# The input product of the odd layer by seven block products instead of eight

## The reference, cut to what matters

```python
h = rmsnorm(x, norm_w[layer])
proj = h @ od_w_in[i]                    # 1024 x 3088
q, k, v, r, a_lr = split_cols(
    proj, [GLA_K_WIDTH, GLA_K_WIDTH, GLA_V_WIDTH, GLA_V_WIDTH, GLA_GATE_RANK])   # 512, 512, 1024, 1024, 16
c_out = gla_mixer(q, k, v, a_lr, gla_w_a2[i], gla_b_a[i], gla_norm[i]) * jax.nn.silu(r)
x = x + c_out @ od_w_out[i]
```

## Time and profile before

| | |
|---|---|
| time, 3 runs | 1682.04 us median, 1680.92 to 1682.89 |
| span of the profiled execution | 1680.7 us, 22631 instructions (no other time of that execution is recorded) |
| granted TensorE clock, mean | 0.998 |
| TensorE / VectorE / ScalarE / GpSimd busy | 98% / 49% / 38% / 17% |
| DMA | 236.18 MB, 141 GB/s |

### The profile page before, as it was taken

The page is one execution under the profiler, slowest core; times in us unless marked ns, Lnnn a source line. Parts: engine busy times, 40 slices in busy tenths (PEclk is TensorE's granted clock), DMA queues, the critical chain, the costliest instruction groups (busy, mean ns, idle before and its releaser), DMA issues.

```text
span 1680.7 us, 22631 instructions
## 1 busy us (share of the span) xinstructions
PE 1643.8 (98%) x7898; PEld 1330.3 (79%) x7898; DVE 822.9 (49%) x1671; ACT 633.7 (38%) x1616; POOL 281.0 (17%) x516
## 2 busy tenths in 40 slices
PE   6999999999999999999999999999999999999998
PEld 4777788777777678888778888888888888878886
DVE  6744545667666574533552333334334443354443
ACT  6522334666666562323450222222222232132221
POOL 3883000000000332100000112222222121000110
PEclk9999999999999999999999999999999999999999
DMA  5466544455444865222243323423332332276663
GB/s 217 146 182 190 152 153 134 142 170 149 146 148 134 262 177 200 83 93 95 79 151 107 114 96 110 129 98 114 115 110 88 129 110 75 94 246 192 189 189 110
DMA packets 224520, 236.18 MB, mean 141 GB/s; under 512 B 53368, under 2 KB 169752, under 8 KB 224408
## 3 DMA queue, kind: packets, MB, share of 16 engines
q1 hardware_dynamic: 221752, 233.07, 43.7%
q10 hardware_dynamic: 2656, 1.67, 0.4%
HBM read 140.12 MB, written 94.57 MB: 140 GB/s over the span
## 4 chain that ended last, share of the span: by engine, by line
PE 92%; DVE 3%; ACT 2%; DMA 2%; issue 1%; SPq 0%; POOL 0%; DVEq 0%; ACTq 0%; POOLq 0%
PE bank L1232 23%; PE bank L2196 22%; PE bank L2246 10%; PE score_banks L2196 8%; PE bank L2355 8%; PE score_banks L2355 2%; PE bank L2305 2%; PE bank L2302 2%; PE bank L2303 2%; PE score_banks L2284 1%; PE score_banks L1288 1%; PE bank L1315 1%; PE bank L1269 1%; PE bank L1261 1%; PE bank L1305 1%
## 5 line engine op out<-in xcount | busy, mean ns | idle before, releaser
L1232 PE MATMUL bank<-ht_hi,ev_w_hi 128*128 128x512 f32 x576 | 239.7, 416 | 2.4 <-DVE ht_lo L944 2.4
L2196 PE MATMUL bank<-ht_hi,odd_w_hi 128*128 128x512 f32 x576 | 239.1, 415 | 0.0
L1232 PE MATMUL bank<-ht_hi,ev_w_lo 128*128 128x512 f32 x576 | 226.4, 393 | 0.0
L1232 PE MATMUL bank<-ht_lo,ev_w_hi 128*128 128x512 f32 x576 | 226.2, 393 | 0.0
L2196 PE MATMUL bank<-ht_lo,odd_w_hi 128*128 128x512 f32 x576 | 225.5, 392 | 0.0
L2196 PE MATMUL bank<-ht_hi,odd_w_lo 128*128 128x512 f32 x576 | 224.1, 389 | 0.0
L1232 PEld LDWEIGHTS bank<-ht_hi,ev_w_hi 128*128 128x128 f32 x576 | 108.8, 189 | 38.7 <-issue 17.1
L1972 DVE COPY odd_stage<-bank 128x512 f32<-128x512 f32 x72 | 49.8, 691 | 168.9 <-PE bank L2196 168.9
L1232 PEld LDWEIGHTS bank<-ht_lo,ev_w_hi 128*128 128x128 f32 x576 | 108.6, 189 | 24.9
L2196 PEld LDWEIGHTS bank<-ht_lo,odd_w_hi 128*128 128x128 f32 x576 | 108.1, 188 | 24.1
L2196 PEld LDWEIGHTS bank<-ht_hi,odd_w_hi 128*128 128x128 f32 x576 | 108.3, 188 | 23.1 <-issue 3.0
(11 more groups left out here) (320 smaller groups left out, 3337.7 us busy)
## 6 DMA issues: line engine op xcount, KB each, us to landing
odd_gl_in<-scr_heads SPq DMA_DIRECT2D x32, 640.0 KB, 4.3
scr_heads<-odd_stage SPq DMA_DIRECT2D x64, 256.0 KB, 2.2
odd_w_raw<-od_w_in SPq DMA_DIRECT2D x24, 512.0 KB, 3.8
ev_w_raw<-ev_w_in SPq DMA_DIRECT2D x17, 512.0 KB, 6.0
ev_s_cos_sin<-scr_s_cos_sin SPq DMA_DIRECT2D x32, 256.0 KB
odd_xo_sum<-x SPq DMA_DIRECT2D x16, 512.0 KB, 4.0
scr_x<-odd_xo_sum SPq DMA_DIRECT2D x16, 512.0 KB, 2.9
scr_gla_mix<-odd_gl_out SPq DMA_DIRECT2D x32, 256.0 KB, 2.1
```

The lines of the kernel that those rows point to most:

```text
L1232: mm = pe.matmul(acc[n % 3], w[j][:, k, :], h[:, k, t], start=(k == 0 and r == 0), stop=(k == KT - 1 and r == 2))
L2196: mm = pe.matmul(acc[n % 4], w[j][:, k, :], h[:, k, t], start=(k == 0 and q == 0), stop=(k == KT - 1 and q == 2))
```

## The change

Twelve pairs of column groups by two halves of the tokens (1024 each) give 24 rounds. In a round the weights are four blocks A of 512x128 (two halves of the depth, two groups) and the turned activations four blocks B of 512x512 (two halves of the depth, two token blocks). The four results C11, C12, C21, C22 of a round come from seven block products of 12 matmuls (`PRODUCTS`) in place of eight, in Winograd's form. It needs

- four sums of weights in each round (S1 to S4), made by GpSimd from raw weights, which are now loaded as 1 MB for a pair and once for each token half. Seven operands of weights are cast and reduced in each round, 128x512 each.
- four sums of activations for each token half (T1 to T4). Those of the first half are made by VectorE (`sum_first`) at the end of the even layer's output product, where the turned rows are now kept raw; seven blocks of 128x2048 are then cast and reduced. The turned rows of the second half are stored in DRAM (`store_turned`). In slots 1 to 9 they are loaded again a quarter at a time, summed by GpSimd (`sums_of_half`) and stored. At slots 45 to 48 the seven blocks are loaded over those of the first half, and cast and reduced.
- combinations of the results: ScalarE copies the first product out of its bank (`copy_first`) before product 3 adds to it, and takes C11 (`take_c11`); VectorE makes six sums (`combine`) in place of four copies.

A round has four slots with 2, 2, 2 and 1 products; there are 96 slots. The linear attention has its 64 steps in slots 13 to 44 and 62 to 93: first all heads for the first half of the tokens, then for the second, with a state for each head. Gates are made from slots 1 and 54 on. The low-rank products have 40 matmuls before slot 0 and 40 in slot 53. The tiles of the even layer's output product now go in the order of the tokens, the gating stage takes the token blocks in the order 2, 3, 0, 1 (`GLU_AT`), and the attention rows of block 0 are loaded there and no longer in the even layer. At the end, the output weights take the places of blocks B11, T2, T3 and B21, and are loaded in slots 93 and 94.

```diff
+GLU_AT = (2, 3, 0, 1)
...
+    N_Q = 12
+    N_IT = 2 * N_Q
+    N_SLOT = 4 * N_IT + 2
+    R_Q = 8
...
+    GLA_AT = (13, 62)
+    GATE_AT = (1, 54)
+    LOW_AT = 53
...
+    NP = 7
+    PRODUCTS = (("A11", "B11"), ("S2", "T2"), ("S3", "T3"), ("A12", "B21"), ("S1", "T1"), ("A22", "T4"), ("S4", "B22"))
+    W_OPS, H_OPS = [w for w, h in PRODUCTS], [h for w, h in PRODUCTS]
+    IN_SLOT = ((0, 1), (2, 3), (4, 5), (6,))
+    W_ORDER = ("A11", "S2", "A12", "S3", "S1", "A22", "S4")
+    W_SPLIT_AT = {1: ("A11",), 2: ("S2", "A12"), 3: ("S3", "S1", "A22"), 0: ("S4",)}
...
+    S_ORDER = ("S1", "S2", "S4", "S3")
...
+    H_LOAD_AT = {45: ("B11", "T2"), 46: ("T3", "B21"), 47: ("T1", "T4"), 48: ("B22",)}
+    H_SPLIT_AT = {46: ("B11",), 47: ("T2", "T3"), 48: ("B21", "T1"), 49: ("T4", "B22")}
...
+        def load_w(i):
+            if i:
+                sp.wait_ge(w_ready, w_ready_0 + 1 + w_no(i - 1, "A22"))
+                sp.wait_ge(s_added, s_no(i - 1, "S3"))
+            q = i % N_Q
+            sp.dma_start(w_raw[:], prm["od_w_in"][2 * q:2 * q + 2].rearrange("g p k n -> p g k n")).then_inc(w_in[i % 2], 16)
...
+        def load_sums(k):
+            if k == 0:
+                for j in range(2):
+                    sp.wait_ge(hb_stored[j], hb_stored_0[j] + 32 * 4)
+                sp.wait_ge(o_full, o_full_0 + NT)
+            else:
+                sp.wait_ge(hb_back, 32 * k)
+            sp.dma_start(tb_in[:], scr["hb"][0:4, :, k].rearrange("o p t -> p o t")).then_inc(hb_in, 16)
...
+        for s in range(N_SLOT):
+            it, j = divmod(s, 4)
+            if j == 0 and 0 < it + 1 < N_IT:
+                load_w(it + 1)
+            for o in H_LOAD_AT.get(s, ()):
...
+            if s in (1, 3, 5, 7):
+                if s > 1:
+                    store_sums((s - 3) // 2)
+                load_sums((s - 1) // 2)
+            if s == 9:
+                store_sums(3)
...
+        for s in range(N_SLOT):
+            it, j = divmod(s, 4)
+            if s and step(s - 1) is not None:
+                inverse(step(s - 1))
+            if even(step(s + 2)):
+                spread(step(s + 2) // 2)
+            if it + 1 < N_IT:
+                for o in {1: ("S1", "S2", "S4"), 2: ("S3",)}.get(j, ()):
+                    weight_sum(it + 1, o)
+            if s in (2, 4, 6, 8):
+                sums_of_half((s - 2) // 2)
...
+        def copy_first(it):
+            act.wait_ge(p_done, product_no(it, "A11"))
+            if it:
+                act.wait_ge(ev_done, ev_no(it - 1, "U4"))
+            else:
+                act.wait_ge(hn_done, hn_done_0 + NT)
+                act.wait_ge(x1_stored[1], x1_stored_0[1] + 16 * (NT // 2))
+            s.copy(u_sum[:], acc_of(it)["C11"]).then_inc(u_copied, 1)
+
+        def take_c11(it):
+            act.wait_ge(p_done, product_no(it, "A12"))
+            if it:
+                k = ROLES.index("C11")
+                act.wait_ge(stored[k], stored_0[k] + 16 * it)
+            s.copy(out_of["C11"], acc_of(it)["C11"]).then_inc(c11_done, 1)
...
+        def combine(it, o):
+            acc = acc_of(it)
+            role = {"U3": "C22", "U4": "C12"}.get(o, o)
+            if o == "U2":
+                dve.wait_ge(p_done, product_no(it, "S2"))
+                dve.wait_ge(u_copied, it + 1)
+                ops = (u_sum[:], acc["U2"], u_sum[:])
+            if o in ("U3", "U4"):
+                dve.wait_ge(p_done, product_no(it, "S3" if o == "U3" else "S1"))
+                dve.wait_ge(ev_done, ev_no(it, "U2"))
+                ops = (out_of[role], acc["U3" if o == "U3" else "C22"], u_sum[:])
+            if o == "C21":
+                dve.wait_ge(p_done, product_no(it, "A22"))
+                dve.wait_ge(ev_done, ev_no(it, "U3"))
+                ops = (out_of["C21"], acc["C21"], out_of["C22"])
+            if o == "C22":
+                dve.wait_ge(ev_done, ev_no(it, "C21"))
+                ops = (out_of["C22"], acc["C22"], out_of["C22"])
+            if o == "C12":
+                dve.wait_ge(p_done, product_no(it, "S4"))
+                dve.wait_ge(ev_done, ev_no(it, "U4"))
+                ops = (out_of["C12"], acc["C12"], out_of["C12"])
...
+        sum_first("T4")
+        lower_first("B21")
+        lower_first("T2")
...
+        split(0, "A11")
+        split(0, "S2")
+        lower_first("T4")
+        take_low(0)
+        split(0, "A12")
+        split(0, "S3")
+        lower_first("T3")
+        split(0, "S1")
+        split(0, "A22")
+
...
+        def product(it, q):
+            w, h = PRODUCTS[q]
+            out_ = ("C11", "U2", "U3", "C11", "C22", "C21", "C12")[q]
+            pe.wait_ge(w_ready, w_ready_0 + 1 + w_no(it, w))
+            if it % N_Q == 0:
+                pe.wait_ge(h_lo_done, h_lo_no(it // N_Q, h))
+            if it == 0:
+                if q < 2:
+                    pe.wait_ge(low_free, 2 - q)
+                if q in (2, 4):
+                    pe.wait_ge(x1_done, x1_done_0 + 2 * NT - 2)
+            if it and q in (0, 1, 2, 4):
+                pe.wait_ge(ev_done, ev_no(it - 1, ("U3", "C22", "C21", None, "C12")[q]))
+            if q == 3:
+                pe.wait_ge(u_copied, it + 1)
+            if q == 5:
+                pe.wait_ge(ev_done, ev_no(it, "U2"))
+            if q == 6:
+                pe.wait_ge(c11_done, it + 1)
+            for k in range(4):
+                for r, (a, b) in enumerate(((w_hi, h_hi), (w_lo, h_hi), (w_hi, h_lo))):
+                    mm = pe.matmul(acc_of(it)[out_], a[w][:, k], b[h][:, k], start=(k == 0 and r == 0 and q != 3),
+                                   stop=(k == 3 and r == 2),
+                                   skip_group_check=(q == 3))
+            mm.then_inc(p_done, 1)
...
+        low_part(0, 0, "B11", True, False)
+        low_part(0, 1, "B11", True, False)
+        low_part(0, 1, "T1", False, False)
+        low_part(0, 1, "B22", False, True)
+        turn_out(NT - 1)
+        low_part(0, 0, "B21", False, True)
+        for s in range(4 * N_IT):
+            it, j = divmod(s, 4)
+            product(it, IN_SLOT[j][0])
+            for k in gates_at(s):
                 if k % GH == 0:
                     gates(k // GH)
-            if is_pair(m + 1):
-                first(m + 1)
-            products(n, KT // 2).then_inc(acc_full, 1)
-            if is_pair(m - 1):
-                third(m - 1)
-            if is_pair(m):
-                second(m)
+            if step(s + 1) is not None:
+                first(step(s + 1))
+            for q in IN_SLOT[j][1:]:
+                product(it, q)
+            if s and step(s - 1) is not None:
+                third(step(s - 1))
+            if step(s) is not None:
+                second(step(s))
+            if s == LOW_AT:
+                low_part(1, 0, "B11", True, False)
+                low_part(1, 0, "B21", False, True)
+                low_part(1, 1, "B11", True, False)
+                low_part(1, 1, "T1", False, False)
+                low_part(1, 1, "B22", False, True)
```

More of the change, by code:

```diff
@@ new lines, in step, with place, gates_at @@
+    def step(s):
+        for half, at_ in enumerate(GLA_AT):
+            if at_ <= s < at_ + n_pair // 2:
+                return n_pair // 2 * half + s - at_
+        return None
+    def place(m):
+        half, r = divmod(m, n_pair // 2)
+        return r // HALF, HALF * half + r % HALF
+    def gates_at(s):
+        return [8 * half + k for half, at_ in enumerate(GATE_AT) for k in (2 * (s - at_), 2 * (s - at_) + 1) if 0 <= k < 8]
+    even = lambda m: m is not None and m % 2 == 0
+    is_r = lambda it: 0 <= it < N_IT and it % N_Q >= R_Q
@@ L1525, in load_x4 @@
         def load_x4(i):
-            h, ii = divmod(i, NBLK)
-            b = ii // 2
+            h, at_ = place(2 * i)
+            ii = at_ // 2
+            half, b = divmod(ii // 2, 2)
             if i >= 2:
@@ L1933, in scalar @@
+            if j == 1 and is_r(it - 1):
+                silu_tanh(it - 1, "C21")
+            if even(step(s_ + 2)):
+                exps(step(s_ + 2) // 2)
+            if s_ and step(s_ - 1) is not None:
+                norm(step(s_ - 1))
+            if step(s_ + 1) is not None:
+                copy_kv(step(s_ + 1))
+            for k in gates_at(s_):
                 if k % 2 == 0:
                     gate(k)
-            if n == 14:
+            if s_ in (GATE_AT[0] + 5, GATE_AT[1] + 5):
```

700 lines of the change are left out of this document (433 added, 267 removed).

## The result

| | before | after |
|---|---|---|
| median of the runs beside one another | 1682.47 us (4 runs) | 1725.41 us (4 runs) |
| span of the profiled execution | 1680.7 us | 1727.1 us (time 1728.96) |
| TensorE busy, mean granted clock | 98%, 0.998 | 93%, 0.974 |

The change makes the kernel slower: ratio 1.0252, 95% interval 1.0229 to 1.0275. I had said 1676 us, 1654 to 1693. By the profiled executions, the span grew by 46.4 us where I had -6.3.

A forecast was written before the change was run, and what follows sets the result against it. The prediction took TensorE (98% busy) as the bound. Its terms, -67.2 + 9.2 + 6.2 + 23.5 + 6 + 8 - 2 + 10, sum to -6.3 us from 1680.7, forecasting 1676 us, range 1654 to 1693.

The forecast's parts named there:

- low clock: Matmuls behind waits for data start at 1.2 GHz: 1.6 us each, about seven waits, +10 us (0 to 14).
- the wheel: Second token half's sums, slots 1 to 9: four turns of load, add, store, about 17 us each; with gates +23.5 us.
- half-way seam: Seven blocks cast and reduced during slots 46 to 51, some of it late: +6 us (0 to 12).
- gating stage: 2 MB of attention leave the full DMA queues at 560 us and return at 580: -2 us (-4 to +3).
- products and restarts: Input product: 288 fewer matmuls at 0.2267 us each, and 16 GLA restarts at 0.1: together -67.2 us.
- low-rank products: 80 matmuls instead of 64; the second 40, at slot 53, have nothing beside them: +9.2 us.
- start of the layer: First product waits for VectorE, 22.6 us after the even layer's last output product instead of 16.5: +6.2 us.
- short slot: Fourth, one-product slot of GLA rounds: 0.65 us left, cost 0; as rival, chain too long, about +17, chance 0.17.
- end: Last product's weights cast in slots 94 to 96, row 1 loaded behind the last gated stores: +8 us (0 to 13).
- wheel would be hidden: Rival: loads and stores land fast and pauses cost no clock: 1658, or 1653 with few cold starts; chance 0.18.
- slower wheel: Rival: loads and weight loads share queues, or GpSimd is slow: +8 to +15, 1684 to 1691; chance 0.15.

The follow-up runs named there:

- the third experiment: Changed kernel with four buffers for the gate rows instead of two: 1712.5 us.
- The eleventh run: Changed kernel with only the 2 MB of attention loaded and multiplied behind the last rows of the gating stream: 1717.7 us.
- the fastest kernel: Changed kernel with seams reordered, four gate buffers, sums in pieces, second-half GLA, gates and low products earlier, T4 buffered separately, sums' transfers first: 1669.4 us, ratio 0.9918.

## Why the prediction was wrong

What the change removes I had right; what failed is the cost of the waits that it adds. The low clock behind them, the wheel's term with a wrong subtraction in it, the half-way seam and the gating stage, where I had a gain, are 36 of the 53 us between my sum and the measured one. By its own terms, predicted and measured in the profiled execution, in us:

| term | said | measured |
|---|---|---|
| products and restarts | -67.2 | -66.7 |
| low-rank products | +9.2 | +9.2 |
| start of the layer | +6.2 | +9.7 |
| wheel, gates | +23.5 | +32.7 (waits 3.7, 6.6, 8.4, 6.7 and, second half, 5.4; gates' matmuls +1.9) |
| half-way | +6 | +14.4 (9.0 at the products, 5.4 at the first GLA pairs) |
| short slot | 0 | +4.4 |
| end | +8 | +9.0 |
| gating stage | -2 | +3.8 |
| even layer | not seen | +4.6 |
| low clock | +10 | +22.2 |
| rest, in GLA's own matmuls | | +3.1 |

The last row closes the sum. The 1.5 us of waits that the kernel before has in this part are not taken off above, so it is that much too small. The 1.9 us of the gates' matmuls are low clock too: behind the waits of 3.7 and 5.4 us each of these two groups takes 2.0 us instead of 1.05. The profiled execution took 1728.96 us, 3.6 above the median of its kernel.

- **What bounds the kernel, the products, the short slot.** Right, for the short slot in the first half. Its slack was 0.65 us by my reading, 0.67 in the trace and 0.76 by the kernel with half of the seventh product. But I read it from a round of the kernel before and took the second half to be like the first; the pairs fall one slot later in it, and that costs 4.4.
- **The start of the layer (3.5 us).** My count had no time for the sums S1 and S2. GpSimd takes 3.2 us for each there, and VectorE waits for S2 with the copies of the low banks behind it.
- **The wheel.** Four waits where I put four; their sum was 25.4 where I had 26.8. The largest, at C11, went by the chain I wrote down. The one at 890 us did not: I had C22 behind S2's rest, and it was a gate row waiting for its store; the third experiment shows mine behind it, 2.9 instead of 5.1.
- **A wrong subtraction in that term.** I took off 4.3 us that "the gates cost before". They are the gate matmuls themselves, 4.3 us of busy time without a wait (the one wait there is 1.2 us), and they are still there, at 6.2 us now. The subtraction and the 1.9 us more are 6.2 of the 9.2 us by which the term is short; the gates' waits, 9.1 where I had 3.4, are the other 3 and more, and the other three waits gave some of it back.
- **The low clock, the largest miss (12 us).** I priced a slow start at 1.6 us, the trace shows 1.5 to 3.1 (once 0.9), and I counted seven where there are eleven: those at 1277 and 1300 us stand behind waits that I had at nothing, that at 1250 behind one that I had at 1 us, and each end wait has its own. At the 1.43 us that my sum comes to, four more are 5.7 us of the miss, and the higher price of all eleven is the other 6.5; the four more are a follow-up cost of the other misses. The Trainium skill (TensorE: Matmul & The Clock Gate, section HAM oscillation) describes a kernel in which every burst behind a wait for data starts cold. The trace agrees in part. In the changed kernel the clock is at its lower level, 1.2 GHz, behind all ten waits of 3.7 us and more, and also behind those of 1.85 and 2.31 us at 1277 and 1300; behind 3.28 us at 559 and 1.54 at 1207 it is not. So the length of a wait alone doesn't tell a short one's price. The kernel without the wheel, with 18.6 us of waits less, has 7.4 less at low clock.
- **Half-way (8 us).** I counted casts and rests one after another, but not that a sum of blocks on VectorE waits 4.2 us at 1184 us for a store behind loads, nor the first pairs of the second half.
- **The gating stage (6 us), wrong in sign.** I took transfers moved out of full queues as a gain and didn't ask what they are moved ahead of. They went ahead of the output weights, ScalarE stood 6.3 us at the cast of one, and the casts of the gating stream stood behind it. The eleventh run shows it: the gating stage is 7.7 us shorter, and the time 8.
- **The even layer (4.6 us).** Not in any term; 3.3 of it are told below. They are of the profiled execution; whether the three faster ones had them, no run shows.
- **The rivals.** That the wheel would be hidden was wrong by its premise: its four turns take 86 us, from 845.2 to 931.2. The slower wheel, +8 to +15, meets the size of that term's miss by luck: the four waits that it would have lengthened were together shorter than forecast. The short slot came true in part, 4 us of its 17, by a cause that it didn't have. None had what came: many waits of 2 to 8 us, most with a cold start.

What stays open: what holds the first pair of the second half for 6.6 us even in the fastest kernel, how much of the 8 us half-way another split of VectorE's work could save, and what the kernel before would gain by the gating stage's new order.

## What to carry to other kernels

A full engine hides its queues' mistakes. Before cutting its work by an eighth, list every in-order queue that feeds it, and for each transfer or step that the change adds ask what stands behind it; here the order of the same work, with smaller pieces and a few more buffers, was worth 56 us, as much as the 57 us of matmuls that the change removes net of the added ones. Price waits together with their slow starts, and read a schedule in every phase that it has, not in one round.

## What the hardware showed that I had not expected

Tiny instructions of VectorE can be held up by GpSimd for as long as large ones. At the end of the even layer, VectorE's steps on 128x4 elements, 0.16 us each before the change (where the burst below catches a later step, 1.32 us at 552.56), in the changed kernel:

```profile
551.45 1.39 DVE L1113 TENSOR_TENSOR ev_at_small<-ev_at_small 128x4 f32<-128x4 f32 x1
552.88 1.57 DVE L1114 TENSOR_TENSOR ev_at_small<-ev_at_small 128x4 f32<-128x4 f32 x1
554.38 1.65 DVE L1115 TENSOR_SCALAR ev_at_small<-ev_at_small 128x4 f32<-128x4 f32 x1
```

```profile
551.17 4.83 POOL L712 TENSOR_TENSOR ht_lo_raw<-ht_lo_raw,glu_g_first 128x512 f32<-128x512 f32 x3 [409.17 <-DMA ht_lo_raw<-scr_gate_a]
```

Each ends about when one of GpSimd's three sums ends. ScalarE waits 7.4 us for them and TensorE 3.3 (the first row of the list of waits). It is a matter of tenths: where GpSimd's burst begins 1.6 us after the first of the three, as in the kernel with half of the seventh product, all take 0.16 and the wait is not there; in the kernel with GpSimd's wheel and in the fastest only one is caught. The Trainium skill (GPSIMD Engine Reference, section Key points) names VectorE's steps with two SBUF inputs, and those in a 2-port mode, as the ones that contend with GpSimd. The trace agrees for the first two, which read two tiles; the third reads one, and no run shows whether it is in such a mode.

So 3 us of an execution of this kernel depend on a race between a transfer and an instruction, and a comparison of two variants carries them along. At the layer's start it goes the other way: beside VectorE's 128x2048 rests GpSimd's sums S1 and S2 take 3.2 us each instead of 1.3. The 3.8 us are about what the first product came too late (3.5); that the one causes the other is read from the queue, not tried.
